# Recurrence levels as narrow tiles, products ahead of differences, a round's outputs in one bank, and output gates emptied first

## The reference, cut to what matters

```
f = lb + (1 - lb) * sigmoid(f_logit);  k = 1 - f;  q = silu(q);  a = cumsum(log f) per chunk
S_t = diag(f_t) S_{t-1} + (1 - f_t) v_t^T;   o_t = S_t^T q_t
in chunks:  o = (q * exp(a)) S + scores v,   scores[t,s] = sum_k q[t] exp(a[t]-a[s]) k[s]  for s <= t
            S = exp(a_last) S + (k * exp(a_last - a))^T v
```

## Time and profile before

| | |
|---|---|
| median of 3 runs | 1558.54 us (1558.11 to 1559.86) |
| profiled execution | 1557.91 us |
| its span | 1556.1 us |
| busy: TensorE, VectorE, ScalarE | 98%, 54%, 45% of the span |
| recurrence, first to last round | 74.56 to 347.65 us of the span |
| rounds begin (first transposes, L927) | 74.56, 142.77, 216.03, 283.99 us |

### The profile page before, as it was taken

The page is one execution under the profiler, slowest core; times in us unless marked ns, Lnnn a source line. Parts: engine busy times, 40 slices in busy tenths (PEclk is TensorE's granted clock), DMA queues, the critical chain, the costliest instruction groups (busy, mean ns, idle before and its releaser), DMA issues.

```text
span 1556.1 us, 23913 instructions
## 1 busy us (share of the span) xinstructions
PE 1526.6 (98%) x10239; PEld 1343.4 (86%) x10239; DVE 839.8 (54%) x1234; ACT 695.9 (45%) x1036; POOL 3.6 (0%) x16
## 2 busy tenths in 40 slices
PE   7999999999999999999999999999999999999998
PEld 7999999999999989988888777778899887778888
DVE  6477776645645656564244676643223566653333
ACT  6565676654333323222233655633122666653332
POOL 0000000000000000000000000000000000000000
PEclk9999999999999999999999999999999999999999
DMA  6212111204323222232323200122322111122322
GB/s 231 82 55 89 55 55 55 69 28 151 109 82 107 83 94 96 82 109 76 102 95 108 50 28 1 55 82 81 108 82 82 55 55 55 55 68 88 102 81 82
DMA packets 130540, 125.44 MB, mean 81 GB/s; under 512 B 20169, under 2 KB 128484, under 8 KB 130052
## 3 DMA queue, kind: packets, MB, share of 16 engines
q1 hardware_dynamic: 129956, 120.36, 23.9%
q0 software_dynamic: 464, 3.56, 0.6%
q10 hardware_dynamic: 16, 0.00, 0.0%
HBM read 119.66 MB, written 4.26 MB: 80 GB/s over the span
## 4 chain that ended last, share of the span: by engine, by line
PE 90%; DVE 5%; ACT 3%; issue 2%; DMA 0%; DVEq 0%; SPq 0%; ACTq 0%
PE PS L841 76%; PE PS L954 3%; PE PS L1168 3%; PE PS L1111 2%; PE PS L1133 2%; DVE wlo L1802 1%; PE PS L1116 1%; PE PS L1117 1%; DVE small L2324 1%; PE PS L1145 0%; ACT whi L1308 0%; PE PS L1118 0%; PE PS L966 0%; PE PS L1002 0%; PE PS L909 0%
## 5 line engine op out<-in xcount | busy, mean ns | idle before, releaser
L841 PE MATMUL PS<-zhi,whi 128*128 128x258 f32 (+2 forms) x1856 | 485.9, 321 | 4.7 <-DVE zlo L1848 3.4
L841 PE MATMUL PS<-zlo,whi 128*128 128x258 f32 (+2 forms) x1856 | 474.4, 314 | 0.0
L841 PE MATMUL PS<-zhi,wlo 128*128 128x258 f32 (+2 forms) x1856 | 473.7, 314 | 0.0
L841 PEld LDWEIGHTS PS<-zhi,whi 128*128 128x128 f32 x1856 | 306.1, 190 | 29.7 <-issue 6.7
L841 PEld LDWEIGHTS PS<-zhi,wlo 128*128 128x128 f32 x1856 | 304.9, 189 | 22.0
L841 PEld LDWEIGHTS PS<-zlo,whi 128*128 128x128 f32 x1856 | 305.0, 189 | 19.3
L1802 DVE TENSOR_TENSOR wlo<-raw,whi 128x2048 fp32r<-128x2048 f32 (+2 forms) x114 | 247.8, 2174 | 118.8 <-ACT whi L1308 118.6
L1308 ACT ACTIVATE whi<-raw 128x2048 fp32r<-128x2048 f32 (+2 forms) x114 | 207.6, 1821 | 146.6 <-DMA raw<-in_w_up 54.5
L1308 ACT ACTIVATE Pm<-PS,small 128x144 f32<-128x144 f32 (+3 forms) x128 | 68.8, 541 | 60.4 <-DVE small L2324 60.1
L2324 DVE TENSOR_REDUCE small<-PS 128x1 f32<-128x144 f32 (+3 forms) x128 | 63.3, 504 | 46.4 <-PE PS L1118 45.1
L841 PE MATMUL PS<-ghi,whi 128*128 128x512 f32 x176 | 69.6, 396 | 0.0
(11 more groups left out here) (352 smaller groups left out, 2142.9 us busy)
## 6 DMA issues: line engine op xcount, KB each, us to landing
raw<-in_w_in SPq DMA_DIRECT2D x50, 1024.0 KB, 5.0
raw<-in_w_up SPq DMA_DIRECT2D x22, 1024.0 KB, 5.1
raw<-in_w_out SPq DMA_DIRECT2D x8, 1024.0 KB, 5.1
raw<-in_w_down SPq DMA_DIRECT2D x8, 1024.0 KB, 5.1
raw<-in_w_br_mla SPq DMA_DIRECT2D x4, 1024.0 KB, 4.9
raw<-in_w_br_fox SPq DMA_DIRECT2D x4, 1024.0 KB, 5.0
raw<-in_w_down SPq DMA_DIRECT2D x4, 768.0 KB, 4.8
hspill<-hT SPq DMA_DIRECT2D x1, 2112.0 KB, 7.4
```

The costliest lines, as they stand in the source:

```text
L841: ins = mm(o_, l_, r_, start=first, stop=last)
```

## The change

Levels 0 to 4 are made in blocks of 32 keys, with 16 moving queries each: one matmul per block, its 32 columns into the partitions of the same block. Level 5 takes the left 32 of each 64, level 6 is as before. The unused parts of the score bank are no longer written. Step i of VectorE makes product i ahead of state update and difference. The chunks 1 to 4 of a round's outputs go side by side into bank 6, chunk 0 into bank 7, and two copies take them out. Rounds 2 to 4 transpose into banks 4 and 5, with no wait on the output copies; level 0 waits for these instead. ScalarE empties an output gate ahead of the step's exponential. Counts of semaphores follow.

```diff
+        def kd_bank(p, hh):
+            return 4 + hh if p else 7 - hh
...
                 if i == 0:
                     pe.wait_ge(mul_ready, 8 * p + 1)
                     e = E[b % 2]
+                    if not p:
+                        pe.wait_ge(norm1.rb_ready, 1)
                     for hh in range(2):
-                        bank = 7 - hh
-                        if p:
-                            if hh == 0:
-                                pe.wait_ge(s_ready, 4 * p)
-                            pe.wait_ge(o_copied, 5 * p)
-                        else:
-                            pe.wait_ge(norm1.rb_ready, 1)
...
+                    if j == 0 and p:
+                        pe.wait_ge(o_copied, 2 * p)
...
-                            m = 64 if j == 6 else P
-                            rhs = e[:, hh, t0:t0 + n].rearrange("p (n b) -> p n b", b=blk)[:, :, half:blk]
-                            ins = mm(PS[0:m, bank, 64 * it:64 * it + 64].rearrange("p (n b) -> p n b", b=half),
-                                     e[:, hh, t0:t0 + m], rhs, start=True, stop=True)
+                            if j <= 4:
+                                for r in range(0, P, 32):
+                                    rhs = e[:, hh, t0 + r:t0 + r + 32].rearrange("p (n b) -> p n b", b=blk)[:, :, half:blk]
+                                    dst = PS[r:r + 32, bank, 64 * it + r // 2:64 * it + r // 2 + 16]
+                                    ins = mm(dst.rearrange("p (n b) -> p n b", b=half), e[:, hh, t0 + r:t0 + r + 32], rhs,
+                                             start=True, stop=True)
+                                continue
+                            if j == 5:
+                                for r in (0, 64):
+                                    ins = mm(PS[r:r + 32, bank, 64 * it + r // 2:64 * it + r // 2 + 32],
+                                             e[:, hh, t0 + r:t0 + r + 32], e[:, hh, t0 + r + 32:t0 + r + 64],
+                                             start=True, stop=True)
+                                continue
+                            ins = mm(PS[0:64, bank, 64 * it:64 * it + 64], e[:, hh, t0:t0 + 64], e[:, hh, t0 + 64:t0 + P],
+                                     start=True, stop=True)
...
                 for c in range(5):
                     t0, n = chunk(c)
-                    bank = 6 + c % 2
                     if c == 0:
                         pe.wait_ge(c0_copied, p + 1)
+                        pe.wait_ge(s_ready, 4 * p + 4)
                     elif c == 1:
-                        pe.wait_ge(s_ready, 4 * p + 4)
                         pe.wait_ge(sc_copied, 8 * p + 8)
-                    else:
-                        pe.wait_ge(o_copied, 5 * p + c - 1)
...
-                        dst = PS[64 * hh:64 * hh + 64, bank, 0:n]
+                        dst = PS[64 * hh:64 * hh + 64, 7, 0:n] if c == 0 else PS[64 * hh:64 * hh + 64, 6, t0 - NM:t0 - NM + n]
...
                 elif i == 9:
-                    for c in range(5):
-                        t0, n = chunk(c)
-                        act.wait_ge(o_done, 5 * p + c + 1)
-                        A_(oT[:, p, t0:t0 + n], PS[:, 6 + c % 2, 0:n], ACT.Copy).then_inc(o_copied, 1)
+                    act.wait_ge(o_done, 2 * p + 1)
+                    A_(oT[:, p, 0:NM], PS[:, 7, 0:NM], ACT.Copy).then_inc(o_copied, 1)
+                    act.wait_ge(o_done, 2 * p + 2)
+                    A_(oT[:, p, NM:T], PS[:, 6, :], ACT.Copy).then_inc(o_copied, 1)
...
+                if kind == "og":
+                    tile_done(act, name)
+                    tile_free(A_(halves(late(og[:, h, :])), acc_late(name), ACT.Silu), name)
                 for step in sorted(hooks, reverse=True):
                     rec_step(*step)
...
-                elif kind == "og":
-                    tile_free(A_(halves(late(og[:, h, :])), src, ACT.Silu), name)
...
                 elif i <= 7:
+                    mul(i)
                     if 2 <= i <= 5:
                         state(i - 2)
                     if i <= 6:
                         sub(i + 1)
-                    mul(i)
                     if i >= 2:
                         evac(i - 2)
```

More of the change, by code:

```diff
@@ L916, in rec_step @@
                     e = E[b % 2]
+                    if not p:
+                        pe.wait_ge(norm1.rb_ready, 1)
                     for hh in range(2):
-                        bank = 7 - hh
-                        if p:
-                            if hh == 0:
-                                pe.wait_ge(s_ready, 4 * p)
-                            pe.wait_ge(o_copied, 5 * p)
-                        else:
-                            pe.wait_ge(norm1.rb_ready, 1)
                         for c in range(4):
                             t0, n = chunk(c)
-                            ins = tr(PS[0:n, bank, P * c:P * (c + 1)], e[:, hh, t0:t0 + n], ident[:, :])
+                            ins = tr(PS[0:n, kd_bank(p, hh), P * c:P * (c + 1)], e[:, hh, t0:t0 + n], ident[:, :])
                         ins.then_inc(kd_turned, 1)
@@ L1004, in rec_step @@
                             ins = mm(dst, Sc[:, hh, c - 1, :], e[:, hh, t0:t0 + n], start=False, stop=True)
-                    ins.then_inc(o_done, 1)
+                    if c in (0, 4):
+                        ins.then_inc(o_done, 1)
             pending = None
@@ L1031, in _ @@
                     if t == 1:
-                        pe.wait_ge(o_copied, 20)
+                        pe.wait_ge(o_copied, 8)
                     elif t >= 2:
@@ L1427, in rec_after @@
                     act.wait_ge(kd_turned, 2 * p + hh + 1)
-                    tick(A_(kdt[0:NM, hh, 0, :], PS[0:NM, 7 - hh, 0:P], ACT.Copy))
-                    A_(kdt[:, hh, 1:4, :], PS[:, 7 - hh, P:4 * P].rearrange("p (c k) -> p c k", c=3), ACT.Copy)\
+                    tick(A_(kdt[0:NM, hh, 0, :], PS[0:NM, kd_bank(p, hh), 0:P], ACT.Copy))
+                    A_(kdt[:, hh, 1:4, :], PS[:, kd_bank(p, hh), P:4 * P].rearrange("p (c k) -> p c k", c=3), ACT.Copy)\
                         .then_inc(kdt_ready, 1)
             def o_square(t):
-                act.wait_ge(o_copied, 5 * (t + 1))
+                act.wait_ge(o_copied, 2 * (t + 1))
                 A_(late(sqo[t]), late(oT[:, t, :]), ACT.Square).then_inc(osq, 1)
@@ L1461, in _ @@
                     if p >= 2:
-                        act.wait_ge(o_done, 5 * (p - 1))
+                        act.wait_ge(o_done, 2 * (p - 1))
                     tile_free(A_(halves(late(qf[p % 2][:, hh, :])), src, ACT.Silu), name)
@@ L1483, in _ @@
                     tile_free(A_(halves(late(dst)), src, ACT.Sigmoid), name)
-                else:
+                elif kind == "pin":
                     tile_free(A_(halves(pin[:, h, PADC:]), src, ACT.Copy), name)
@@ L1925, in free @@
                         if p:
-                            dve.wait_ge(o_done, 5 * p)
+                            dve.wait_ge(o_done, 2 * p)
                     elif x == 2:
@@ L2089, in _ @@
                     if p >= 2:
-                        dve.wait_ge(o_done, 5 * (p - 1))
+                        dve.wait_ge(o_done, 2 * (p - 1))
                     f, k_ = av[p % 2][:, hh, :], kf[p % 2][:, hh, :]
```

## The result

| | before | after |
|---|---|---|
| median of the runs beside each other, us | 1559.2 (1558.11 to 1560.15, 4 runs) | 1541.45 (1540.88 to 1543.19, 4 runs) |
| profiled execution, span, us | 1556.1 | 1539.1 |
| round 1, 2, 3, 4, us | 68.21, 73.26, 67.96, 63.66 | 63.74, 71.73, 63.82, 56.60 |
| TensorE's idle ahead of level 3, rounds 1, 2, 3, us | 0.57, 0.67, 0.67 | 2.18, 4.00, 2.55 |

The ratio is 0.9891, 95% interval 0.9879 to 0.9902: 17.7 us less by the medians, 17.0 by the spans. The four rounds give 17.2 of it (4.47, 1.53, 4.14 and 7.06). 1540.5 was forecast.

The account below looks back on a forecast made before the run. TensorE was taken to bound round 4, with chains through ScalarE and VectorE limiting earlier rounds. Rounds saving 5.6, 1.35, 5.25 and 5.8 us sum to 18.0, from 1557.9 to 1539.9, median 1540.5; 8-in-10 range 1533 to 1555.

Parts of the forecast that it names:

- Narrow levels: TensorE, levels 0 to 5: 64 records in 0.6 us; levels 0 to 3 save 1.0 us each, 4 and 5 about 0.85.
- the rival of tiles one at a time: Four column groups don't overlap, so a level's records take 4.0 us: about 41 us more, 1600 us; chance 0.07.
- The forget chain: ScalarE and VectorE, rounds 1 to 3: 9.2 us between forget sigmoids, 7.4 to level 3; saves 2.2, 0.55, 1.85.
- The clock: Round 2: TensorE idles up to 3.6 us ahead of level 3; a clock fall there costs at most 1.5 us.
- The pool run: Round 2, VectorE's 21.6 us run: level 6 begins 27.0 us after level 3 instead of 26.6, 0.4 lost.
- No gain of its own: Emptying output gates early gains nothing itself; without it late exponentials would hold TensorE a further 1 to 2 us.
- The outputs: Round ends, outputs in one bank: 0.7 us saved in rounds 1 and 3, 1.2 in round 2, 0.1 in round 4.
- Program order: Rival: groups start only in program order, 1.2 us a level; 11.9 us saved, 1546.6 us; chance 0.12.
- the floor per record: Rival: no record follows another in under 0.025 to 0.030 us; 3.6 us saved, 1555 us; chance 0.13.
- a chain that does not bind: Rival: VectorE and ScalarE keep up in the forget chain; 30 us saved, 1528 us; chance 0.08.

Follow-up runs that it names:

- e7_f_first: The changed kernel with ScalarE also emptying a forget tile (sigmoid, then logarithm) ahead of the step's exponential: 1531.61 us.
- e3_narrow_only: The kernel before the change with the narrow levels added and nothing else: 1542.01 us.
- e1_diff_first: The changed kernel with VectorE's step in the old order, level products behind state and difference: 1539.92 us.
- e10_transposes_back: The changed kernel with the transposes of rounds 2 to 4 in the output banks again, waiting for the output copies: 1542.62 us.
- e8_pool_run: e7_f_first plus, in round 2, obhi ahead of the weight copy in two output-gate steps and two low weight copies behind VectorE's run: 1527.20 us.
- e4_gates_late: The changed kernel with the output gates' accumulators emptied behind the exponentials again: 1544.27 us.
- e9_by_turns: The changed kernel with a round's outputs in two banks by turns, five copies, each product waiting for the copy two before: 1541.66 us.
- e5_group_by_group: The changed kernel with levels 0 to 4 ordered by column group, all matmuls of one 32-column group before the next: 1550.81 us.
- e6_tiles64: The changed kernel with tiles of 64 keys in levels 0 to 5, 32 records in two groups instead of 64 in four: 1545.38 us.

## Why the prediction was right, and where its sizes were off

**Narrow levels.** The step was right, the size low. 0.6 us was taken for 64 records by a pace of 0.037 for one record in one group; the trace has 0.55 to 0.58 at 0.032. The 0.25 taken for leaving the narrow form was 0.11. A level with its state product is 1.23 us (1.34 for the first) in place of the forecast 1.45, levels 4 and 5 are 0.67 and 0.63 in place of 0.95. Round 4, all TensorE, gave 7.06 where 5.8 stood: 5.0 for levels 0 to 3 (4.0), 2.1 for levels 4 and 5 (1.7), 0.18 for the outputs (0.1), less 0.2 of large products a little longer. Two of its sums do not come out of their own terms: a level's add to 1.42, not 1.45, and levels 4 and 5 save 0.80 each, not 0.85; a third, the rival of tiles one at a time, comes to 38 to 40 us in place of 41. None of them moves the forecast by more than half a us.

**The forget chain.** 9.2 us from sigmoid to sigmoid, 7.4 on to level 3: the trace has 9.2 (9.21, 9.23, 9.22) and 7.43. Level 3 came 2.18, 0.48 and 1.86 us earlier in rounds 1, 2 and 3 than before, forecast 2.2, 0.55 and 1.85. e7_f_first proves the chain: taken away, the waits of 2.2 to 4.0 are at most 0.3. What the prediction did not see is that the sigmoid needs the same move as the output gates. Nor did it price this chain with narrow levels and the old order: e3_narrow_only reaches level 3 of round 2 at 31.22 us, 1.35 before the changed kernel. Of that 0.6 goes with the products' new place (e1_diff_first), and about 0.8 is what the end of round 1 gained, which level 3 of round 2 does not pass on (e10_transposes_back, where it comes at 31.71).

**The clock is the term that was mis-sized.** The prediction let it fall in round 2 alone, where VectorE hides it, and the trace shows that too: behind that fall TensorE still waits 1.0 and 1.6 us for VectorE, at levels 5 and 6. But its own sum gave idles of over 2 us in rounds 1 and 3 as well, where behind level 3 TensorE is what bounds. There the fall cost 1.5 each. Behind level 3 these rounds were to save 3.4 (2.7 and 0.7); levels and outputs gave 3.97 in round 1, less 1.54 for the slow product and 0.14 of others: 2.29. The two errors nearly cancel: the clock took 3.1 us over two rounds, and all the rest gave 2.3 more than forecast, most of it the levels; so the rounds gave 17.2 in place of 18.0. The mechanism was right, but that the total came within 1 us is partly luck.

**The pool run.** Level 3 to level 6 took 26.75 us (27.0 forecast, 26.6 before) with oblo 5.03 behind level 3 (5.2). e8_pool_run shortens this run and round 2 shortens by the same. "No gain of its own" for the early gates holds, and e4_gates_late shows what they prevent: 2.8 us by the medians, above the 1 to 2 put on it.

**The outputs.** 0.71, 1.19, 0.70 and 0.18 less at the ends of the rounds, forecast 0.7, 1.2, 0.7 and 0.1. The cause was put wrongly in part: the prediction saw the gain in the chunks' waits and said that the transposes' other banks add no wait. They take one away, and it is the larger: 0.5 of the 0.7 (e9_by_turns), while 0.8 comes back when they are undone (e10_transposes_back).

**The rivals.** Program order and the floor per record are out: 7 ns between groups, 0.55 us for 64 records, round 4 better than forecast. In the level shown above the last record of L947 starts behind three of L957, so records of different groups do pass each other, though by e5_group_by_group this reaches no further than about two matmuls. The Trainium skill ("TensorE: Matmul & The Clock Gate", Part 3) says that matmuls are strictly first in, first out; these records do not bear that out. The Trainium skill's floor of about 25 ns from start to start (same page, Part 1) is not borne out between groups (7 ns); within one group the steps seen keep it: 39, 25 and 25 ns for L946's and L947's records of 16 columns, 32 ns for 32 columns. Small tiles one at a time and a chain that does not bind are refuted by the same rows and by e7_f_first.

**What stays open.** When the clock falls, and what exactly lets a record pass an earlier one: no run varies that alone. The clock fell behind 2.18, 2.55 and 4.00 us of idle in the changed kernel, but not behind 2.19 in e9_by_turns or 2.61 in e1_diff_first, and not behind 1.53 in e8_pool_run or 1.3 in e6_tiles64, though behind 1.8 in e4_gates_late; after 2.5 to 2.6 it lasted 3.4 us in some and 6.8 in others, and in e3_narrow_only it began before the wait was over. Its cost here is known, its rule is not.

## What to carry to other kernels

When one engine's work shrinks, write down the chain that the other engines run through the same step and see where it becomes the longer one: here the narrow levels paid 1.2 us each where TensorE bounds and, with the other edits in place, nothing up to level 3 of round 2. Then the cheapest next edit can be one instruction's place, as here the forget tile's sigmoid ahead of an exponential that waits for another engine (10 us). Edits that pay alone can pay little beside another (the three other edits here 4.5 us with wide levels, half a us with narrow ones), so each is tried both ways. Price every new idle of TensorE twice: for itself, and for the clock behind it, here 1.5 to 2.6 us wherever TensorE bounds next.

## What the runs showed of the hardware

- Float32 matmuls in four groups of 32 columns run side by side if they alternate in the program: starts 7, 7 and 6 ns apart, a set every 32 ns (changed kernel, level 4 of round 4). With the same matmuls group after group the overlap is lost but for the last three records of each (e5_group_by_group, 1.70 us in place of 0.55).
- In one column group a float32 record of this kind takes 32 ns with 32 columns (changed kernel) and 58 ns with 64 (e6_tiles64), whether 16 or 32 columns move through the 32-column one (levels 0 to 4 and level 5 keep the same pace).
- A fall of the granted clock to 0.50 (1.2 GHz) at an idle lasted 3.4 us and cost 1.5 us of a product stream (changed kernel, rounds 1 and 3); where it lasted 6.8 us it cost 2.6 (e3_narrow_only); with further waits inside it, it lasted 10.2 us (e4_gates_late).
